# The chunked delta rule of the mixer, recast from 128x128 block matrices to 64-column chunk matrices on quarters of the array

## The reference, cut to what matters

```python
CHUNK = 64
def gated_delta_chunked(q, k, v, g, beta, s0):
    ...
    gc = jnp.cumsum(blocks(g), axis=-1)
    decay = jnp.exp(jnp.where(tri_incl, gc[..., :, None] - gc[..., None, :], -jnp.inf))
    kb = kc * bc[..., None]
    lmat = jnp.where(tri_strict, jnp.einsum('nbhik,nbhjk->nbhij', kb, kc) * decay, 0.0)
    tinv = lax.linalg.triangular_solve(eye + lmat, eye, left_side=True, lower=True, unit_diagonal=True)
    u = jnp.einsum('nbhij,nbhjv->nbhiv', tinv, vc * bc[..., None])
    w = jnp.einsum('nbhij,nbhjk->nbhik', tinv, kb * jnp.exp(gc)[..., None])
    intra = jnp.einsum('nbhik,nbhjk->nbhij', qc, kc) * decay
    qd = qc * jnp.exp(gc)[..., None]
    kd = kc * jnp.exp(gc[..., -1:] - gc)[..., None]
    def step(s, inp):
        u_i, w_i, a_i, qd_i, kd_i, gl_i = inp
        v_new = u_i - jnp.einsum('bhck,bhkv->bhcv', w_i, s)
        o = jnp.einsum('bhck,bhkv->bhcv', qd_i, s) + jnp.einsum('bhij,bhjv->bhiv', a_i, v_new)
        s = s * gl_i[..., None, None] + jnp.einsum('bhck,bhcv->bhkv', kd_i, v_new)
        return s, o

def bidir_gated_delta(q, k, v, beta, g, s0_fwd, s0_bwd):
    o_f, s_f = gated_delta_chunked(q, k, v, g[:, :, 0], beta[:, :, 0], s0_fwd)
    ...  # the same on the flipped sequence
    return o_f + fl(o_b), s_f, s_b
```

## Time and profile before

| | us |
|---|---|
| median of 3 runs | 3506.57 (3506.3 to 3511.83) |
| the profiled execution's own time | 3500.1 |
| its span | 3498.2 |
| PE busy in the span | 3060.3 |
| DVE busy | 1179.3 |
| ACT busy | 584.9 |
| POOL busy | 239.8 |
| mean granted clock of PE | 0.913 |

### The profile page before, as it was taken

The page is one execution under the profiler, slowest core; times in us unless marked ns, Lnnn a source line. Parts: engine busy times, 40 slices in busy tenths (PEclk is TensorE's granted clock), DMA queues, the critical chain, the costliest instruction groups (busy, mean ns, idle before and its releaser), DMA issues.

```text
span 3498.2 us, 32724 instructions
## 1 busy us (share of the span) xinstructions
PE 3060.3 (87%) x12891; PEld 1680.6 (48%) x12891; DVE 1179.3 (34%) x2536; ACT 584.9 (17%) x1262; POOL 239.8 (7%) x366
## 2 busy tenths in 40 slices
PE   6995688878998888876988889999999887999998
PEld 4554578764433333333454544444444555444443
DVE  3616454544411111133844424530038443211001
ACT  2103332310111111102221221100022212200000
POOL 0000000000111111110200000100012100000000
PEclk9987899989999999997998589999999985999999
DMA  5113422114499999752110015631212010222221
GB/s 203 49 48 129 161 73 73 49 61 174 160 394 408 403 409 403 310 235 107 49 49 25 25 48 186 217 120 73 74 62 74 25 49 0 91 72 72 72 78 43
DMA packets 138013, 468.23 MB, mean 134 GB/s; under 512 B 15325, under 2 KB 28283, under 8 KB 111751
## 3 DMA queue, kind: packets, MB, share of 16 engines
q1 hardware_dynamic: 118047, 415.14, 31.2%
q0 software_dynamic: 18912, 50.36, 3.9%
q10 hardware_dynamic: 904, 0.66, 0.1%
HBM read 459.76 MB, written 26.28 MB: 139 GB/s over the span
## 4 chain that ended last, share of the span: by engine, by line
PE 45%; DVE 6%; ACT 2%; issue 1%; SPq 0%; DMA 0%; POOLq 0%; POOL 0%; ACTq 0%; DVEq 0%
PE ps_l L2312 38%; PE ps_l L2788 2%; PE ps_l L76 1%; DVE pT_notsel_l L2765 1%; DVE small_l L2763 1%; PE ps_l L3088 1%; PE ps_l L2990 1%; DVE pT_notsel_l L2755 1%; PE ps_l L2870 0%; DVE small_l L3107 0%; PE ps_l L159 0%; PE ps_l L2475 0%; ACT work_l L2851 0%; DVE hT_l L2489 0%; PE ps_l L2997 0%
## 5 line engine op out<-in xcount | busy, mean ns | idle before, releaser
L2312 PE MATMUL ps_l<-ring_l,hT_l 128*128 128x512 f32 (+3 forms) x1280 | 542.7, 572 | 11.8 <-ACT arena_l L2605 7.2
L2312 PE MATMUL ps_l<-hT_l,ring_l 128*128 128x512 f32 (+2 forms) x1152 | 478.8, 575 | 14.8 <-DVE hT_l L2489 13.4
L2312 PE MATMUL ps_l<-ring_l,arena_l 128*128 128x512 f32 x1024 | 440.2, 592 | 2.8 <-DVE arena_l L3256 2.8
L2312 PEld LDWEIGHTS ps_l<-ring_l,hT_l 128*128 128x128 f32 x1280 | 251.7, 207 | 233.0 <-issue 197.8
L2312 PEld LDWEIGHTS ps_l<-hT_l,ring_l 128*128 128x128 f32 x1152 | 213.8, 192 | 271.1 <-issue 247.8
L1833 PE MATMUL ps_m<-w_m,gatheredT_m 128*64 128x512 f32 (+1 forms) x784 | 291.8, 637 | 46.5 <-issue 42.0
L2312 PEld LDWEIGHTS ps_l<-ring_l,arena_l 128*128 128x128 f32 x1024 | 194.3, 190 | 248.0 <-issue 243.5
L1833 PEld LDWEIGHTS ps_m<-w_m,gatheredT_m 128*64 128x64 f32 (+1 forms) x784 | 102.6, 162 | 174.1 <-issue 169.4
L360 PE MATMUL ps_a<-arena_a,ring_a 128*128 128x512 f32 (+1 forms) x448 | 168.3, 539 | 0.9 <-DVE arena_a L508 0.9
L2528 DVE SCALAR_TENSOR_TENSOR small_l<-small_l 128x1 f32<-128x1 f32 x16 | 2.5, 159 | 452.4 <-ACT work_l L2518 452.4
L1833 PE MATMUL ps_m<-hT_m,gatheredT_m 128*64 128x512 f32 (+1 forms) x272 | 132.0, 642 | 18.7 <-issue 18.4
(11 more groups left out here) (529 smaller groups left out, 3652.5 us busy)
## 6 DMA issues: line engine op xcount, KB each, us to landing
ring_l<-in_mlp_w SPq DMA_DIRECT2D x32, 2048.0 KB, 8.1
w_m<-in_exp_w_gate SPq DMA_DIRECT2D x49, 1024.0 KB
w_m<-in_exp_w_up SPq DMA_DIRECT2D x49, 1024.0 KB
w_m<-in_exp_w_down SPq DMA_DIRECT2D x49, 1024.0 KB, 13.4
ring_a<-in_mod_w SPq DMA_DIRECT2D x12, 2048.0 KB, 8.2
pT_notsel_l<-in_mod_w POOLq DMA_DIRECT2D x24, 1024.0 KB, 5.6
ring_a<-in_w_mod SPq DMA_DIRECT2D x9, 2048.0 KB, 8.5
hT_m<-in_exp_w_gate SPq DMA_DIRECT2D x17, 1024.0 KB
```

What stands on the lines that cost most here:

```text
L2312: mm = pe_.matmul(out, lhsT, rhs, start=start, stop=stop)
```

## The change

The matrices of 64 x 64 are now held one chunk above the other: the upper 64 partitions have the first chunk of the tile, the lower 64 the second, and a matrix of four heads takes 256 columns instead of 512. The two directions lie side by side, so one array of 512 columns (and one PSUM bank) holds both (`sq64`, `rows`). A matmul on such matrices has 64 rows and 64 columns: it uses a quarter of the array, and the two chunks use the two quarters of the diagonal. In detail:

- `setup_pe`: gate and keys as 16 quarter matmuls each for both directions together. With outputs, the gate in full width for `qd` is made apart by 8 full matmuls. `query_pe` follows once ACT has read the gate's bank.
- DVE multiplies decay by beta, and makes `lt`, `mt` and the first inverse, for both directions in one instruction each; `intra` takes two. The constants hold the masks as chunks.
- `m` and `mt` lie next to each other (`m_of`, `mt_of`). `second_pe` makes both updates, one by `t1` stationary and one by `mt` stationary, and DVE subtracts both in one instruction (`second_dve`). Only the first inverse is still turned (`turn_pe`, `turned_act`). The last level makes `mt` alone.
- u is no longer made for itself: `value_pe` adds the inverse times v and minus w times state in one PSUM bank, and ACT copies that out. The recurrence handles one chunk of each direction at a time in one bank. DVE decays both states in one instruction (`decay_dve`, ahead of time) and adds both increments in one (`state_dve`).
- The steps are shifted: while the recurrence of step `s` runs, the setup and the first two levels of step `s + 1` stand between its parts, on all three engines.
- The side products of `later` run at levels 3 and 4 instead of 1 and 3, ahead of the second product of direction 0; the next level's matmuls wait for their copy.
- Ahead of the steps: the gates' columns are copied per step and direction (7 copies by ACT instead of 1), the chunk decays in 4 copies by DVE instead of 1, and the setup waits until both first side products are copied out.

```diff
-        def bank(d, n):
-            return PS[:, 3 * d + n, :]
+        TB, UB, VB, OB, DB = 0, 2, 4, 5, 6
...
+        def first_pe(s, l, d):
...
+            for h in range(4):
+                for c in range(2):
+                    mm = pe_.matmul(PS[rows(c), TB + d, sq64(0, h)], lt[rows(c), sq64(d, h)], m_of(s, d)[rows(c), sq64(0, h)], start=True, stop=True)
+        def second_pe(s, l, d):
+            pe_.wait_ge(t1_ev[d].sem, (INV - 1) * s + l)
+            if d == 0 and l in LATER_LEVELS:
+                later.pe(PS[:, TB, :])
+            for h in range(4):
+                for c in range(2):
...
+                    mm = pe_.matmul(PS[rows(c), UB + d, sq64(0, h)], t, mt, start=True, stop=True)
+            if l < INV - 1:
...
+                        mm = pe_.matmul(PS[rows(c), UB + d, sq64(1, h)], mt, t, start=True, stop=True)
+        def keys_pe(s):
...
+                        mm = pe_.matmul(PS[:, UB + c, sq64(d, h)], kg[rows(c), d * 512 + h * P:d * 512 + (h + 1) * P],
+                                        mt_of(s, d)[rows(c), sq64(0, h)], start=True, stop=True)
+        def value_pe(s, n):
...
+                    pe_.matmul(PS[rows(c), VB, hh(h)], mt_of(s, d)[rows(c), sq64(0, h)], vtok[rows(c), TILE_AT[d][s], hh(h)],
+                               start=h == 0, stop=False, skip_group_check=True)
+            pe_.wait_ge(w_ev.sem, s + 1)
...
+                    mm = pe_.matmul(PS[rows(c), VB, hh(h)], wt[:, c * 512 + sq64(d, h).start:c * 512 + sq64(d, h).stop], state[d][:, hh(h)],
+                                    start=False, stop=True, skip_group_check=True)
...
+        def state_pe(s, n):
+            pe_.wait_ge(vn_ev.sem, 2 * s + n + 1)
...
         def delta_pe():
...
             for _ in range(2):
-                later.pe(PS[:, 7, :])
-            for s in range(NTA):
+                later.pe(PS[:, VB, :])
+            pe_.wait_ge(later.copied.sem, 8)
+            for s in range(-1, NTA):
+                new, old = s + 1 <= LAST, s >= 0
+                if new:
+                    setup_pe(s + 1)
+                if old:
+                    value_pe(s, 0)
+                if new and with_out(s + 1):
+                    query_pe(s + 1)
+                if old:
+                    state_pe(s, 0)
+                if new:
+                    turn_pe(s + 1)
+                    for d in range(2):
+                        first_pe(s + 1, 1, d)
+                if old:
+                    value_pe(s, 1)
+                if new:
+                    for d in range(2):
+                        second_pe(s + 1, 1, d)
+                    for d in range(2):
+                        first_pe(s + 1, 2, d)
+                if old:
+                    state_pe(s, 1)
+                if new:
+                    for d in range(2):
+                        second_pe(s + 1, 2, d)
+                    for l in range(3, INV):
+                        for d in range(2):
+                            first_pe(s + 1, l, d)
+                        for d in range(2):
+                            second_pe(s + 1, l, d)
+                    keys_pe(s + 1)
...
+        def second_dve(s, l, d):
+            dve_.wait_ge(up_mm[d].sem, (INV - 1) * s + l)
...
+            n = 512 if l < INV - 1 else 256
+            w = mm2[s % 2][:, d * 512:d * 512 + n]
+            dve_.tensor_tensor(w, w, PS[:, UB + d, 0:n], ALU.subtract).then_inc(up_ev[d].sem, up_ev[d].up())
```

517 lines of the change are left out of this document (312 added, 205 removed).

## The result

| | before | after |
|---|---|---|
| median of the runs | 3506.44 (3501.34 to 3511.83) | 3373.65 (3367.01 to 3376.43) |
| profiled execution; its span | 3500.1; 3498.2 | 3371.15; 3369.4 |
| start of the stage (first setup) | 377.96 | 371.21 |
| length of the stage | 374.5 | 244.3 |
| of it at half clock (1.2 GHz) | 44.4 | 21.1 |

The ratio is 0.9618, with a 95% interval of 0.9597 to 0.964: 134 us less by it, where 131.6 had been forecast. The stage ends with the last two sums of outputs (DVE L1186, 614.09 + 1.40 = 615.49). Its time at half clock is added up from windows of 1 us by their granted clock.

The account below looks back on a forecast made before the run. PE was taken to bound the levels, but not the setup. First inverse 33, steps 35.5, 37 and 3 x 41.6, last recurrence 11.4 and 1.2 ahead gave 242.9 against 374.5: median 3375 us, range 3345 to 3430.

Parts of the forecast that it names:

- The price of a quarter: PE's quarter matmuls in the stage: the two diagonal quarters overlap, 0.030 us a record, with bounds 0.028 and 0.058.
- The first rival: Quarters run one after another on PE: 0.058 us a record, stage 344.8 with the start, 3477 in all; chance 10%.
- The level: One level of the inverse, both directions sharing the engines: 3.4 us where 5.4 stood; levels 3 and 4 start 5.3 apart.
- A step with outputs: Step with outputs on both sides, in PE's order: 38.6 us plus 3.0 for changes of shape, 41.6 where 64.9 stood.
- A change of shape: PE switching between full, half and quarter operands: 0.2 us each, 15 in a step with outputs, 3.0 in all.
- Steps 0 and 1: Step 0, without outputs on either side, 35.5 us including a 1.9 wait for DVE; step 1, in between, 37.
- The first inverse: Ahead of the steps, with no recurrence beside it: 33 us, 9.6 of it before the levels.
- stay hidden: The ring's loads, 2 x 2 MB in a step of 41.6 us, need 8.2 each and cause PE no wait.
- The recurrence beside the inverse: In the steps, the recurrence adds no wait of its own; without other records there, some 5 us more a step.
- The sum: First inverse, steps and last recurrence total 241.7 us, 242.9 with work ahead, against 374.5: 131.6 less.
- The second rival: PE's clock falls to half during quarter matmuls, each PE price doubles: stage 429 us, 3561 in all; chance 10%.
- The third: Longer chain behind DVE and ACT: order costs 8 us in five steps, 3415; 14%, shared with a quarter-stage clock fall.

Follow-up runs that it names:

- sequence A: Changed kernel with idle small matmuls ahead of the first setup: here two diagonal quarters in turn, writing one bank; 0.030 us a record.
- E: In the same run as sequence A: all four quarters in turn, a bank for each row half; 0.016 us a record.
- the profile of the micro sequences: Changed kernel with 48 full matmuls and nine sequences of small ones, results unread, ahead of the first setup; 3402.49 us, stage 236.5.
- the small loads: Changed kernel with the side products' weight loads in the stage cut to an eighth of each tile; 3356.18 us, ratio 0.9559, stage 233.4.
- the last kernel: Changed kernel plus paced loads, four quarters, side products in PE's waits, the other branch's work moved, 12 idle matmuls; 3334.77 us, ratio 0.9512.

## Why the prediction was right

- **The price of a quarter** decided it, and it held: forecast 0.030 by halving the 0.064 of L2870's halves, measured 0.029 in the levels and 0.030 by itself. Halves and longer quarters were put at 0.060 and measured 0.059 to 0.060. The first rival, quarters one after another, would have had 0.057, which is what a single quarter takes. (Its total adds up to 345.2 by its own terms, not 344.8; nothing hangs on it.) On the rule that different row tiles cannot access the same PSUM bank simultaneously (the Trainium skill, TensorEngine Tiling (Array Packing), Restrictions and Gotchas): sequence A breaks it to the letter, in one bank on different partitions, and was as fast (0.030) as the same in two banks (0.029). With the same partitions no run tried it; there E used two banks.
- **The level**: forecast 3.4, and 5.3 with a side product; measured 5.34.
- **A step with outputs**: forecast 41.6, measured 40.3, 40.7 and 39.5 at full clock. A change of shape costs 0.17, not the 0.2 taken from the L900 and L908 rows: with 15 of them 0.45 too much. Of the 0.7 for DVE being late at level 3 about 0.3 came: PE waits 0.54 there, and 0.25 in the levels behind. Two terms too large by a little.
- **Steps 0 and 1**: forecast 35.5 and 37, measured 37.8 and 37.2, with part of each at half clock (windows at 0.91 and 0.96). The forecast wanted 1.00 "but for the first inverse". At full clock, in the profile of the micro sequences, they take 35.1 and 35.8, a little less than forecast, so the half clock made 2.7 and 1.4 us of them.
- **The first inverse**: forecast 33, measured 38.2. PE's wait for DVE's setup, 5.6, was in it; the clock at half for 7 us from 379 on and for 3 more at its end, and a hole of 1.2 during a load, were not. This is the largest miss of a term: with the small loads, without the hole and the second fall, the same inverse took 34.7. The prediction's "stay hidden" for the ring's loads is the step that failed here: PE never waited for their data in the stage, but it stood up to 1.2 us for its own instructions while they ran.
- **The recurrence beside the inverse**: said to hide "some 5 us" a step. Undone, it cost 14.3 us of the stage over five such places, 2.9 each. The step that failed is the size of the waits that it covers: in plain order PE stood 9.4 us more for DVE's setup in the whole stage (15.0 against 5.6) and hardly more for anything else, and 3.4 us more were at half clock. It did not touch the sum.
- **The sum**: 241.7 for the six steps (242.9 with what was put ahead of them) against 244.3. The first inverse and steps 0 and 1 took 7.7 us more than forecast, the steps with outputs 4.3 and the last recurrence 0.8 less. That it is so close is in part luck: the sum was made for full clock, and by the price of half clock the same stage would take 229 there, some 12 us less than forecast. Terms that were too large made up for a clock that was left out. The forecast also set a full-clock stage against one that had 44 us of half clock. The profile was to be 131.6 shorter and is 129.0 shorter: 130.2 in the stage, 6.75 ahead of it and minus 8 behind it, which come and go between executions.
- **The second rival**, the clock: it fell, for 21 us and not for most of the stage. Quarters by themselves kept 2.4 GHz (three whole steps at 1.00), against what the rival feared; what came before each fall was PE standing, 5.6 us for DVE or 0.9 to 1.2 for its instructions, though not every such hole brought a fall. **The third**, a longer chain: no wait on L1160 or L1174 above 0.6 us.

## What to carry to other kernels

Two or four small products on separate quarters of PE, issued in turn, cost half or a quarter of what one quarter costs; lay out operands so that neighbours differ in rows, in columns or in both (0.030 for two quarters of either kind), and give the two row halves that meet in one column half a bank each, as was done here; one bank for both was not tried. When a shorter chain gives no time, look at the granted clock by windows before giving the edit up: here half clock cost 0.70 us for each us, and several of its falls stood behind holes in PE during 2 MB loads that had nothing to do with the edit. Cut and spread loads that are due a whole step later, and put idle matmuls into a long wait that can't be shortened.

## What the runs showed of the hardware that was not expected

- Four quarters in turn: 0.016 us a record, against 0.030 for two and 0.057 for one. Even blocks of eight records on one quarter can overlap in part with the next block (0.036; in another place not, 0.055).
- PE can stand for 1 to 2.4 us in the middle of a loop without any wait, while loads keep all DMA engines busy (share 1.01 to 1.05). Each such hole ends 1.2 to 1.6 us after a 16 KB packet of PE's instructions. With loads an eighth as large none was left; with the same loads in four spaced pieces none over 0.7 us, but with four quarters and spaced pieces, where PE runs faster, one of 1.4 us came back.
- Small edits can move where the clock falls, and one that shortens PE's work can lose all it won: 51 us at half clock with four quarters, 21 without, and none in the last kernel, in which PE's waits were shorter and filled.
